# Residual rows on VectorE, whole-width read-out, norms shared with ScalarE, and another chunk order at stage ends

## The reference

```python
# first network, layer 0: gla_mixer, layer 1: chunk_attention
u = x * (1.0 + sc1) + sh1
y = gla_mixer(u, ...)  if i == 0 else chunk_attention(u, ...)
x = layer_norm(ALPHA * x + (1.0 + g1) * y, ln_g[i, 0], ln_b[i, 0])
u = x * (1.0 + sc2) + sh2
y = squared_relu_mlp(u, ff_w1[i], ff_w2[i])        # width 4096
x = layer_norm(ALPHA * x + (1.0 + g2) * y, ln_g[i, 1], ln_b[i, 1])
# second network, one layer
h = h + hybrid_mixer(rmsnorm(h, norm_mix_g), ...)
h = h + conv_ffn(rmsnorm(h, norm_ffn_g), ...)      # width 2816
return rmsnorm(h, norm_final_g)
```

## Time and profile before

| | us |
|---|---|
| median of 3 runs | 1175.83 |
| lowest, highest | 1174.56, 1180.85 |
| the profiled execution | 1175.19 |
| its span | 1173.5 |
| TensorE busy | 1040.6 |
| VectorE busy | 843.0 |
| ScalarE busy | 501.3 |
| GpSimd busy | 118.7 |

### The profile page before, as it was taken

How to read it: one execution, slowest core, us unless ns; L and a number is a source line. 1 busy time by engine, 2 the same in 40 slices (tenths; PEclk the granted TensorE clock), 3 DMA queues, 4 the chain that set the end, 5 groups by cost and what they waited for, 6 DMA issues and landing times. The chain is left out here.

```text
span 1173.5 us, 16595 instructions
## 1 busy us (share of the span) xinstructions
PE 1040.6 (89%) x6736; PEld 930.0 (79%) x6736; DVE 843.0 (72%) x1155; ACT 501.3 (43%) x690; POOL 118.7 (10%) x156
## 2 busy tenths in 40 slices
PE   0789987999999898884999999689999979999995
PEld 0778976898988787763898998488888969999994
DVE  4678898888778977749755655856876666777775
ACT  0555424333342554534334333244245544555552
POOL 3001204300000451005000000000000000000000
PEclk9989997999999899986999999789999989999998
DMA  9848774778768565312655554244343444556551
GB/s 341 329 178 320 287 292 178 286 262 299 278 250 310 199 249 198 126 47 79 216 187 178 208 176 149 91 165 145 108 144 112 141 137 136 194 180 195 171 191 37
DMA packets 35052, 227.95 MB, mean 194 GB/s; under 512 B 4096, under 2 KB 4224, under 8 KB 10144
## 3 DMA queue, kind: packets, MB, share of 16 engines
q1 hardware_dynamic: 25232, 167.01, 40.9%
q0 software_dynamic: 9744, 59.87, 13.8%
HBM read 225.82 MB, written 1.05 MB: 193 GB/s over the span
## 5 line engine op out<-in xcount | busy, mean ns | idle before, releaser
L1328 DVE TENSOR_TENSOR weight_lo<-weight_raw,weight_hi 128x2048 fp32r<-128x2048 f32 (+2 forms) x187 | 366.6, 1964 | 117.9 <-ACT weight_hi L973 117.9
L400 PE MATMUL ps<-act_hi,weight_hi 128*128 128x256 f32 x1400 | 355.7, 292 | 23.5 <-DVE act_lo L1401 14.7
L973 ACT ACTIVATE weight_hi<-weight_raw 128x2048 fp32r<-128x2048 f32 (+2 forms) x168 | 299.6, 1786 | 152.9 <-PE ps L400 119.6
L400 PE MATMUL ps<-act_lo,weight_hi 128*128 128x256 f32 x1400 | 350.6, 288 | 0.0
L400 PEld LDWEIGHTS ps<-act_hi,weight_hi 128*128 128x128 f32 x1400 | 275.5, 197 | 35.5 <-issue 24.9
L400 PEld LDWEIGHTS ps<-act_lo,weight_hi 128*128 128x128 f32 x1400 | 275.8, 197 | 3.6 <-issue 1.0
L400 PE MATMUL ps<-act_hi,weight_lo 128*128 128x256 f32 x1400 | 186.8, 283 | 0.0
L400 PEld LDWEIGHTS ps<-act_hi,weight_lo 128*128 128x128 f32 x1400 | 175.5, 191 | 0.2
L1348 DVE SCALAR_TENSOR_TENSOR ada_acc<-ada_raw,c_act,ada_acc 128x2048 f32<-128x2048 f32 x42 | 98.6, 2348 | 11.4 <-DMA ada_raw<-ada 9.4
L400 PE MATMUL ps<-weight_hi,mlp_hi 128*128 128x512 f32 x256 | 101.8, 398 | 0.5 <-ACT weight_hi L973 0.5
L400 PE MATMUL ps<-weight_hi,mlp_lo 128*128 128x512 f32 x256 | 101.8, 398 | 0.0
(11 more groups left out here) (303 smaller groups left out, 1344.6 us busy)
## 6 DMA issues: line engine op xcount, KB each, us to landing
weight_raw<-weights SPq DMA_DIRECT2D x144, 1024.0 KB, 5.0
ada_raw<-ada POOLq DMA_DIRECT2D x48, 1024.0 KB, 6.4
weight_raw<-weights SPq DMA_DIRECT2D x23, 512.0 KB, 3.6
row_g<-ln_rows POOLq DMA_DIRECT2D x4, 512.0 KB, 4.0
row_b<-ln_rows POOLq DMA_DIRECT2D x4, 512.0 KB, 6.2
att_bias<-rel_bias POOLq DMA_DIRECT2D x16, 128.0 KB, 3.9
square<-ada_rows POOLq DMA_DIRECT2D x3, 512.0 KB, 4.1
dev<-x_in SPq DMA_DIRECT2D x1, 1024.0 KB, 10.8
```

The lines of the kernel that those rows point to most:

```text
L400: return e.matmul(o, a, b, start=start, stop=False, skip_group_check=True)
L973: e.activation(weight_hi[h][:, 0:size], weight_raw[r][:, 0:size], ACT.Copy).then_inc(hi_full[h], 1)
L1328: ins = e.tensor_tensor(weight_lo[h][:, c], weight_raw[r][:, c], weight_hi[h][:, c].bitcast(F32), ALU.subtract)
```

## The change

1. `residual` moves from GpSimd's program to VectorE's: for each token half `dev * ALPHA * ln_g`, then `ln_b * ALPHA +` that, two `scalar_tensor_tensor` of 128x1024 each, issued after the third split of each MLP and, in attention, between the second and third split, where two ada chunks now come after the splits.
2. At seams 0, 2 and 4 the turned rows of both token halves lie side by side in PSUM (`turned_pair`), and `input_hi` and `input_lo` work on 128x256 tiles after both are turned. Seams 1 and 3 stay by halves.
3. ScalarE normalises three of the four half rows (`norm_rows`, `scale_rows`), VectorE the fourth; for the layer norm VectorE first writes a shift, -mean times root (`ln_shift`). VectorE takes up the next part of y instead of waiting for GpSimd's power.
4. In `last_rows` and at the end, normalisation and row products are merged or reordered.
5. The last up projection of each MLP and of the conv FFN comes before the third last down product; the weights lie in that order, and the splits follow it.
6. In `tail` bank n = 0 is finished before n = 1 is begun. GpSimd's gate row loads wait for the residues instead of the norms.

```diff
         def turned_tile(at, t, k):
-            return ps[:, turn_bank(at, t, k // 4), k % 4 * P:(k % 4 + 1) * P]
+            if at in BY_HALF:
+                return ps[:, TURN_BANKS[at][2 * t + k // 4], k % 4 * P:(k % 4 + 1) * P]
+            return ps[:, TURN_BANKS[at][k // 2], k % 2 * S + t * P:k % 2 * S + (t + 1) * P]
...
         def up_chunk(m, i):
-            return MLPS[m][2] + max(2 * i - 1, 0)
+            n = MLPS[m][0]
+            return MLPS[m][2] + (2 * n - 4 if i == n - 1 else max(2 * i - 1, 0))
...
-            return MLPS[m][2] + (2 * i + 2 if i < n - 1 else 2 * n - 1)
+            return MLPS[m][2] + (2 * i + 2 if i < n - 3 else n + i)
...
                 for n in range(2):
                     rows_of(j2, at, 0, n, b_hi, b_lo, b0, nk, False, False)
-                e.wait_ge(lo_full[j2 % N_SPLIT], j2 // N_SPLIT + 1)
-                for n in range(2):
+                    if n == 0:
+                        e.wait_ge(lo_full[j2 % N_SPLIT], j2 // N_SPLIT + 1)
                     rows_of(j2, at, 0, n, b_hi, b_lo, b0, nk, False, True).then_inc(y_bank, 1)
...
-                for i in range(2, n_blocks):
+                for i in range(2, n_blocks - 1):
                     down(i - 2)
                     project(up_chunk(m, i), up_use(m, i))
+                project(up_chunk(m, n_blocks - 1), up_use(m, n_blocks - 1))
+                down(n_blocks - 3)
...
+            def input_hi(at):
+                for k in range(KT):
+                    if k % 4 == 0:
+                        e.wait_ge(x_turned, 4 * at + 3 + k // 4)
+                    scale, bias, func = modulation(at, k)
+                    if k % 4 < 2:
+                        e.activation(act_hi[:, k, :], turned_pair(at, k), func, bias=bias, scale=scale).then_inc(hi_in, 1)
+                        e.activation(square[:, k, :], turned_pair(at, k), func, bias=bias, scale=scale).then_inc(hi_in, 1)
+                    else:
+                        e.wait_ge(full_in, FULL_AT[at] + k // 4 * 2 + k % 4 - 1)
+                        e.activation(act_hi[:, k, :], square[:, k, :], ACT.Copy).then_inc(hi_in, 1)
...
+            def norm_rows(at, t, n):
+                z = dev_rows[:, t, n * HALF:(n + 1) * HALF]
+                e.wait_ge(shift_in, SHIFT_AT[at] + t + 1)
+                e.activation(z, z, ACT.Identity, bias=row_root[:, t, 2:3],
+                             scale=row_root[:, t, 1:2]).then_inc(act_normed, 1)
...
-            for j in range(J_OUT0 + 2, J_OUT0 + 6):
+            for j in range(J_OUT0 + 2, J_OUT0 + 5):
                 split_hi(j)
-            input_hi(0, 0)
-            input_hi(0, 1)
+            for n in range(2):
+                norm_rows(0, 0, n)
+            split_hi(HELD[0])
+            norm_rows(0, 1, 1)
+            input_hi(0)
...
+            def ln_first(at):
+
+                ln_variance(0, [ln_part(at, 0, n) for n in range(2)])
+                step = ln_part(at, 1, 0)
+                ln_shift(at, 0)
+                ln_variance(1, [step, ln_part(at, 1, 1)])
+
+            def ln_second(at):
+                ln_shift(at, 1)
+                z = dev_rows[:, 1, 0:HALF]
+                e.tensor_scalar(z, z, mean_var[:, 1, 0:1], row_root[:, 1, 1:2], ALU.subtract, ALU.mult).then_inc(normed, 1)
...
+            def residual(idx):
+
+                e.wait_ge(ln_rows_in, 32 * (idx + 1))
+                e.wait_ge(normed, idx + 1)
+                e.wait_ge(act_normed, 3 * idx + 3)
+                i = [own.of(e.scalar_tensor_tensor(out=res[:, t, :], in0=dev_rows[:, t, :], scalar=ALPHA, in1=row_g[:, :],
+                                                   op0=ALU.mult, op1=ALU.mult)) for t in range(ST)]
+                for t in range(ST):
+                    e.wait_ge(dve_step, i[t])
+                    e.scalar_tensor_tensor(out=res[:, t, :], in0=row_b[:, :], scalar=ALPHA, in1=res[:, t, :], op0=ALU.mult,
+                                           op1=ALU.add).then_inc(x_in_place, 1)
...
+            for n in range(2):
+                split_lo(J_ATT + 2 + n)
+            residual(1)
+            for n in range(2):
+                split_lo(J_ATT + 4 + n)
             for _ in range(ATT_ADA[0]):
                 ada_chunk()
-            for n in range(4):
-                split_lo(J_ATT + 2 + n)
...
+            ln_variance(0, [ln_part(3, 0, n) for n in range(2)])
+            step = ln_part(3, 1, 0)
+            last_rows(0)
+            step = [step, ln_part(3, 1, 1)]
+            square_root(3, 0)
+            ln_variance(1, step)
             split_lo(HELD[3])
-            last_rows(1, ln_norm(3, 1, steps + [ln_part(3, 1, 1)]))
-            rms_half(3, 1)
-            input_lo(3, 1)
+            last_rows(1)
+            input_lo_half(3, 0)
+            square_root(3, 1)
+            rms_second(3)
+            input_lo_half(3, 1)
...
             e.wait_ge(final_row_in, 16)
             last_half(0)
-            add_part(5, 1, 1)
+            square_root(5, 1)
             last_half(1)
...
             load_gate_row(1)
             load_ln_rows(0)
-            residual(0)
+            load_ada(3)
             load_ln_rows(1)
-            load_ada(16)
+            load_ada(13)
...
-            residual(1)
             load_ln_rows(2)
```

More of the change, by code:

```diff
@@ L2211, in mlp @@
         out = [up[0]]
-        for i in range(1, n):
+        for i in range(1, n - 1):
             out += [up[i], down[i - 1]]
-        return out + [down[-1]]
+        return out[:-1] + [up[-1]] + down[-3:]
     parts += mlp(a["ff_w1"][0], a["ff_w2"][0])
@@ L2236, in _weights @@
     parts.append(up[0])
-    for f in range(1, FT2):
+    for f in range(1, FT2 - 1):
         parts += [up[f], down[f - 1]]
-    parts.append(down[-1])
+    parts[-1:] = [up[-1]] + down[-3:]
     out = np.zeros((len(parts), P, CW), np.float32)
```

267 lines of the change are left out of this document (141 added, 126 removed).

## The result

The changed kernel takes 1145.85 us (median of four runs, 1141.84 to 1150.61); the kernel before, run beside it, 1178.15 (1174.56 to 1180.85). The ratio is 0.9729, with a 95% interval of 0.9676 to 0.9783: faster by 2.2 to 3.2%. The forecast was 1144.7, in a range of 1139 to 1154.

What follows compares the result with a forecast made beforehand. TensorE, busy 1040.6 of 1173.5 us, was taken as the bound, its idle time mostly at seams between stages. Gains of 3.9 + 0.5 + 11.8 + 5.0 + 4.5 + 4.8 = 30.5 us turned 1175.2 into 1144.7, range 1139 to 1154.

Steps and rivals of the forecast that it cites:

- A: Seam ahead of the first MLP: TensorE restarts at 187.6 instead of 191.52 us, 3.9 us gained.
- B and attention: Seam at 395.5 us and the attention stage behind it: 0.5 us gained, between -5 and +2.5.
- C: Seam at 553.3 us, ahead of the second MLP: residual work off GpSimd, 11.8 us gained including 0.8 from bank order.
- D: Seam at 767.8 us, behind the second MLP: second restart at 763.8 for 767.75, plus 1.0 of clock; 5.0 us gained.
- E: Seam ahead of the conv FFN: restart at 962.0 for 966.52 us, 4.5 us gained.
- F: End of the kernel: last wait 1.7 us instead of 3.86 at full clock, final add earlier; 4.8 us gained.
- rival (2): Seam C: its residues are slow by themselves, total 1153 us; chance 3%.
- near 394: Sign at seam B: a TensorE restart expected near 394 us.
- (1): VectorE and ScalarE absorb part: attention's residual set paid in full (5 us), extra handovers at A, C, E; 1151 us; 20%.
- (3): Clock is kept at A, D, E as the gaps shrink: up to 5 us more gained, 1140 us; 10%.
- (4): Attention: ada loads lose their lead, VectorE's chain grows by 51 us, total 1196 us; 3%.
- (5): Early starts at seams eaten by weights coming no sooner; only F's tail and C's interference stay (13 us), 1162 us; 4%.

Runs made afterwards that it cites:

- e4: Changed kernel with every set of residual rows computed twice (same result); 1150.48 us, 0.976 of before.
- e6: Changed kernel with all four normalised half rows of the layer norms at A, B and C written by VectorE; 1150.42 us, 0.9768 of before.
- e12: Changed kernel with D's half 0 read-out earlier, attention's residual rows earlier, masks before ada loads, two ada chunks before the last split; 1135.94 us.
- e9: Changed kernel with read-out by token half at A, C and E, all four half rows normalised first; 1151.02 us, 0.9789 of before.
- e3: Kernel before with only the residual rows moved to VectorE; 1171.74 us, 0.9943 of before.
- e1: Changed kernel with residual rows back on GpSimd, at C ahead of the gate row load; 1154.62 us, 0.980 of before.
- e2: Changed kernel with residual rows back on GpSimd, at C after the gate row load; 1151.58 us, 0.9772 of before.
- e11: Changed kernel with, at D alone, half 0 read out before half 1's squares and last rows; 1141.68 us, 0.9706 of before.
- e5: Changed kernel with the old chunk order at the end of the three stages, weights and splits likewise; 1150.24 us, 0.9772 of before.
- e8: Changed kernel with GpSimd's two bias masks ahead of the two ada loads as attention begins; 1144.58 us, 0.9716 of before.

## Why the prediction was right, and where not

The forecast took 30.5 us off a kernel at 1175.2; between the medians it is 32.3. That 1144.7 lies only 1.2 us from the measured 1145.85 is in part chance, since the kernel before came out at 1178.15 beside it, and since errors of both signs cancel in the sum.

The ledger, from the growth of the lead between rows of the two traces:

| term | forecast | measured | to which row |
|---|---|---|---|
| start | 0 | 0.5 | the GLA stage's last waits |
| A | 3.9 | 3.8 | A's restart |
| clock behind A | 0 | 0.5 | first relu of MLP 0 |
| B and attention | 0.5 | 1.1 | attention's last wait |
| tail's bank order at C | 0.8 | 0.9 | y(0,0) of C, at full clock |
| low clock ahead of it | 0 | -1.5 | y(0,0) of C |
| C | 11.0 | 11.2 | first relu of MLP 1 |
| D | 5.0 | 6.8 | the mixer's last chunks |
| E | 4.5 | 4.4 | E's restart |
| F | 4.8 | 4.6 | end of the span |
| sum | 30.5 | 32.3 (32.4 from the rounded spans) | |

The bank order is read from attention's last wait to y(0,0): 19.76 us before and 18.85 in e4, e6 and e12, all at full clock. The changed kernel's profile, at 0.84 there, has 20.40.

**A and E** came as worked out. The restart at A was put at 187.6 and came at 187.18, of which 0.5 is the start. That ScalarE's half rows take 0.81 us and its wide activations 0.57, where 0.6 and 0.46 were taken from the earlier trace rows, changed nothing: VectorE's chain beside them is the longer one. The sum did not say how A's gain divides; e6 and e9 do, 1.4 for the norms and 3.1 for the read-out, each with the other in place.

**C.** The lead grew by 10.2 us from y(0,0) to the restart and by 1.0 in the first chunk, which takes 8.2 us (8.7 was assumed). With the bank order that makes 12.1 for 11.8. The cause, GpSimd, is shown by e3 (23.95 to 17.02), and so rival (2) falls.

The Trainium skill (SBUF — State Buffer, Who interferes with whom) has a VectorE instruction with two SBUF inputs contend with any GpSimd instruction that reads SBUF. These runs agree for GpSimd's two-input passes, which VectorE waited out (2.20 and 2.13 us for a 0.69 us instruction), and only in part for its one-input scaling pass: an instruction that began 0.5 us into it took 1.41 us for 0.69, one that began 1.8 us into it its usual 2.28.

**B and attention** came near by terms that were each off. B gave nothing where 0.9 and 1.5 were forecast: y(0,0) is taken 1.9 us sooner after the restart at A, but from there to the restart the chain is 11.36 us where it was 9.98, since y(1,1) now goes ahead of the first read-out. The first softmax is 0.9 us later after the second restart than before, where 0.5 was forecast, by the mask that was named. And the interference of GpSimd with the softmax instructions was worth 2.0 us (from the first softmax to attention's last wait 93.24 us before, 91.27 after), not 1.0: three scalings of scores that take 0.29 or 0.35 us alone took 1.59, 0.73 and 0.66 before. e3, which moves the residual rows alone, shows 1.3 of it; with the residual rows on GpSimd in the changed kernel it is 94.33 (e1) and 93.79 (e2). The bounds of -5 to +2.5 held. The sign "near 394" for B's second restart took the 1.5 us from the 395.5 of before and left out the 3.9 of A; with both it is near 390, and it came at 390.69.

**The residual sets** take 4.55 us from first to last, four of 1.22 us, where 5.0 was assumed. They are free in both MLPs, as e4 shows by doubling them. In attention a doubled set is paid in full (e4), but the set itself costs about 0.3 us at the first softmax (e1), since VectorE would wait there for ScalarE's split. So ahead of the first softmax the stage does not go at VectorE's pace alone, as the prediction had it ("as the stage goes at VectorE's pace, only this counts"); ScalarE's split is close behind. Its 9.1 us "with waits for ScalarE, plus 5.0 of residual" added up what in part covers itself.

**D** was under-sized by 1.8. The first restart came 0.7 later than before against the first relu of MLP 1 (forecast 1.0), the second 5.3 sooner (4.0). y(0,0) was taken 3.2 us sooner after the first relu, where 2.7 were forecast, and from the first restart to the second it took 9.7 us, at a clock that rose on the way, where the forecast had 10.8. Behind the second restart the clock was never low, which gave 1.6 and not the 1.0 of the forecast. That ScalarE's queue holds the first read-out was seen; e11 shows that this hold, with VectorE's, costs 1.6 us at the second restart. B's second restart also found the full clock, which was not forecast; its 1.6 us up to the first scores (18.24 us for 19.86) were lost again by the first softmax, which waited for VectorE and the mask.

**F.** The last wait is 1.72 us at full clock, the forecast's 1.7, and e5 shows the chunk order alone to be worth 2.3 of the waiting and its clock, and 1.7 behind it. The remaining 0.8 (16.59 us before, 15.78 in e5, from the last wait's end to the end of the span) is left, by difference, for the final add that goes ahead of the first half's output, put at 1.3; no run has it alone.

**The rivals.** (1), which had the most weight beside the forecast, did not come: the set in attention costs about 0.3 us (e1), and the interference gained there outweighs it. (3) came in part, at B, D and F but not at A, C and E, where the restart still begins at the low clock. The other traces have the full clock at A twice (e2, e8) and at E twice (e1, e12). (4) would show as waits for an ada load in attention; there is none in VectorE's timeline there. (5) falls with A's 4.3 us still there at B.

What stays open: why the low clock falls at a place in some traces and not in others. From the last GLA waits to y(0,0) of A it is 19.0 us in seven of the thirteen later profiles and 20.4 to 21.8 in the other six (before: 19.3); how much of the scatter of the times this makes is not shown. How the gains of D and E divide between ScalarE's rows and the rest was not tested either.

## What to carry to other kernels

Take a second engine's bulk work off the stretch where VectorE is the chain, or expect each of its passes to hold one instruction up, those with two tensor inputs for nearly their whole length; and look for such overlap wherever a group's mean in one place is a multiple of the same group's elsewhere. When a queue is freed, list every holder of the next instruction before counting the gain: here removing one of three gave 0.3 us, another 1.0, and all three 1.9. And at a seam with two halves, read out what is turned before you finish the rows of the other half, but normalise both before you read out if the next matmul needs both.

## What the hardware showed beyond what was expected

- GpSimd's two-input passes hold not only VectorE's instructions with two SBUF inputs: in e1 the norm of 128x512, a `tensor_scalar` with one, took 2.43 us beside such a pass, 0.54 otherwise. Not every instruction that reads SBUF is held: in the kernel before, a `tensor_reduce` of 128x128 scores took its usual 0.28 us at 416.84, inside the pass of 414.74. GpSimd pays as well: beside the split of 550.82 in e2, which took 4.51 us instead of 2.29, its pass of 553.25 took 4.36, against 2.41 to 2.5 for the same pass in other places.

```profile
538.53 2.43 DVE L1548 TENSOR_SCALAR dev<-dev,mean_var,row_root 128x512 f32<-128x512 f32 x1
...
538.34 2.34 POOL L2146 TENSOR_TENSOR res<-dev,row_g 128x1024 f32<-128x1024 f32 x1
```

- The same idle gap can be followed by either level of the clock. B's second restart comes after a wait of 1.75 us in both kernels, behind a projection that ran at 0.81 before (385.4 to 394.0) and at 0.79 after (380.5 to 388.5), and began at 0.57 before and at 1.00 after. At attention's last wait the length and the level go together: in the ten traces in which it is 3.36 or 3.37 us long, 0.84 follows, as in the changed kernel; in the four with 2.86 to 3.23 us (before 3.06, e4 3.23, e6 2.98, e12 2.86) 1.00 follows. Which of the two brings the other no run shows. So 1.5 us of a difference between two profiles can be this alone, and it has to be looked for before the difference is put down to an edit.
